# Attention's output projection turned to channels on the partitions, router logits summed before the norm, the residual kept in PSUM, a ninth weight slot

## The chip, the cores and the metric

The kernel runs on one core of one Trainium2 chip. The metric is the device time of one execution in microseconds, the median of three runs. The engines are named as in the profile: PE (TensorE matmul), PEld (its weight load), DVE (VectorE), ACT (ScalarE), POOL (GpSimd), SP (SyncE, which here only issues transfers).

## The reference

A batch of 256 tokens with 1024 channels goes through a first block (gated branches and a feed-forward layer) and then through a second block with attention and a mixture of 32 experts. All data is float32. What the change touches is the end of the attention and all that follows:

```python
    mixed = jnp.concatenate([_rmsnorm(o_dil, g_dil_out[layer]),
                             _rmsnorm(o_sb, g_sb_out[layer])], axis=-1)
    x = x + gate_mix[:, None, :] * (mixed @ w_out[layer])
    h2 = _modulate(_rmsnorm(x, g_ffn[layer]), shift_ffn, scale_ffn).reshape(b * s, d)
    y = _hierarchical_moe(h2, w_group[layer], w_expert[layer],
                          w_gate[layer], w_up[layer], w_down[layer]).reshape(b, s, d)
    x = x + gate_ffn[:, None, :] * y
return _rmsnorm(x, g_final)
```

`o_dil` and `o_sb` are the outputs of two kinds of attention, 8 heads of 64 channels each. `_hierarchical_moe` takes group logits (4) and expert logits (32) of each token from `h2`, picks the best group, in it the two best experts, weighs them by a softmax, and adds `(silu(x @ w_gate) * (x @ w_up)) @ w_down` of those two experts. `_modulate(h, shift, scale)` is `h * (1 + scale) + shift`; `gate_mix`, `shift_ffn` and the others are six rows of 1024 numbers, computed from a condition vector.

## The kernel before, in words

`program` writes one instruction stream for each engine by hand (`tensor`, `scalar`, `vector`, `gpsimd`, `sync`); each engine runs its stream strictly in the order in which it is written and waits on semaphores. Nothing is scheduled by a planner.

Up to the end of the attention the weights come as 127 units of 1 MB (`raw`, four buffers). ACT rounds a unit to a high part (line 971), POOL subtracts to get the low part (line 1961), and PE makes three products of each pair (lines 446 to 448: high by high, high by low, low by high), so one unit of 1024 x 256 weights costs 48 matmuls. There are three buffers (NSP = 3) for the two parts of a unit.

The rows of modulation numbers lie in `ADA`. Sums over partitions (`mc_mm`, line 651) put 16 columns of them on partitions, and the helper `spread` (line 660) copies eight blocks of 512 numbers to all partitions, three blocks ahead of the transposes of X (line 673), four ahead of the norm of the attention's input, and one inside the attention. ACT takes each block back to SBUF (line 1207).

The attention runs in two halves of heads. It ends with the value products of the second half (lines 732 to 734), counted by `dv_mm`; DVE divides by the softmax sums (line 1753), ACT squares all four pieces (line 1312) and takes a root, DVE makes four diagonal matrices (line 1773), PE multiplies them in (line 806), ACT and DVE round the result to `xah` and `xal` (lines 1002, 1399), and PE applies the four units of `w_out_2` token by token (`token_major`). DVE multiplies by the gate and adds to X (lines 1789, 1791). Then follow, one after another: the sum of squares and root of X (ACT 1328), the normed and modulated tokens H2 (DVE 1800, 1803), their transpose (PE 821), the copy to HT (ACT 1332, DVE 1810), the logits (PE 832), the choice of experts (DVE 1815 to 1869), the ranks of the tokens in their experts (PE 839 to 841, DVE 1872, 1875), a selection matrix for four experts (DVE 1886), the gathering of their tokens (PE 857), and the first expert (PE 874).

Each expert's weights are three transfers of 2 MB (`EXPERT_WEIGHTS`: two for gate and up, one for down), 96 in all, into a ring of eight slots of 4096 numbers a partition. SP issues them in order (line 2016). The first eight wait until their memory is free (two on `dv_mm`, two on raw buffers, three on the buffers of parts, the last on H2); each later one waits until the transfer eight places before has been used. An expert x runs as `gate_up(x)`, `turn(x-1)`, `scatter(x-2)`, `down(x-1)` on PE. ACT and DVE each copy a half of an expert's output (lines 1362, 1936), and `scatter` (line 921) adds it to four PSUM banks that stay until the end. Every fourth expert is preceded by the gather of the next four.

After the last expert DVE multiplies the sum by the gate and adds X (lines 1944, 1947), a branch on `FLAG` follows (`general`, the way for experts with over 32 tokens), and a last block takes the norm (ACT 2036, 2038), DVE scales (lines 2048, 2050) and SP stores (line 2057).

Of the kernel before, what the change touches and what calls it, by code (L numbers as in the profile page):

```python
# [9 lines left out]
I32 = mybir.dt.int32  # L10
# [5 lines left out]
D = 1024  # L16
# [10 lines left out]
def constants():  # L27
# [15 lines left out]
    put("iota", np.tile(np.arange(32)[None], (128, 1)))  # L43
# [65 lines left out]
def stream_plan():  # L109
# [57 lines left out]
    for n in range(4):  # L167
        whole("w_out_2", "w_out_2", 256 * n, by_rows)
# [8 lines left out]
    for a in range(len(units)):  # L177
        if units[a].half:
# [7 lines left out]
           ("c_2", 8), ("g_mix_2", 8), ("g_dil_out_2", 4), ("g_sb_out_2", 4), ("g_sgu_v", 8), ("b_sgu_v", 8),  # L186
# [11 lines left out]
def program(nc, I, out, const_at):  # L198
    with ExitStack() as ctx:
# [25 lines left out]
        SM = at("SM", 2392, 640)  # L225
# [13 lines left out]
        def ar(off, n, k=None):  # L239
# [23 lines left out]
              for p in range(2)]  # L263
# [9 lines left out]
        MR = ADA[:, 2048:6144].rearrange("p (k n) -> p k n", k=4)  # L273
# [8 lines left out]
        GF2 = ar(8704, 1024)  # L282
        TMPX = at("tmp4", O_XB, 1024)

        H2 = ar(6144, 2048, 2)
        HT = k8(at("ht", O_XA, 2048))
        SLOT = ([at(f"slot{n}", TOP - 8192 + 4096 * n, 4096) for n in range(2)] +
                [at(f"slot{n + 2}", O_RAW + 4096 * n, 4096) for n in range(5)] + [at("slot7", O_XB, 4096)])
        NS = len(SLOT)
        RT = at("RT", 3032, 72).rearrange("p (t n) -> p t n", t=2)  # L290
        WC = at("WC", 3104, 64).rearrange("p (t n) -> p t n", t=2)
        AS, RK, WL = (at(n, 3168 + 64 * i, 64).rearrange("p (t n) -> p t n", t=2)
                      for i, n in enumerate(("AS", "RK", "WL")))
        FLAG = at("FLAG", 3360, 1, I32)
# [4 lines left out]
        GFI = ar(4096, 1024)  # L299
        YP = [ar(8192 + 1024 * n, 1024) for n in range(2)]  # L300
        HE = [ar(10240 + 128 * n, 128) for n in range(2)]
        XG = [k8(at(f"xg{n}", O_XA + 2048 + 1024 * n, 1024)) for n in range(2)]
# [11 lines left out]
        def tap(k, c):  # L314
# [10 lines left out]
        MC = small(16)  # L325
        mx, den = small(16), small(16)
        mx3, den3 = (v.rearrange("p (t h) -> p t h", t=2) for v in (mx, den))
        sso, sh = small(4), small(2)
        gm, gs = small(2), small(2)
        GE, G1 = small(8).rearrange("p (t g) -> p t g", t=2), small(8).rearrange("p (t g) -> p t g", t=2)  # L330
        hot1, hot2, tmp32 = (small(64).rearrange("p (t g) -> p t g", t=2) for _ in range(3))
        m1, m2, dd = small(2), small(2), small(2)
        ixs = [small(2) for _ in range(3)]
        over, left = small(1), small(1)
        so = small(2)
# [5 lines left out]
        d_ws, d_gmp, d_ada, d_gfp, d_p, d_wr, d_gf2, d_gfi, d_out = (sem(n) for n in (  # L341
            "d_ws", "d_gmp", "d_ada", "d_gfp", "d_p", "d_wr", "d_gf2", "d_gfi", "d_out"))
# [4 lines left out]
                 ("norm3", 4), ("heads", 8))  # L347
# [7 lines left out]
         sbs_mm, sv_mm, di_mm, dt_mm, dv_mm, o_mm, rt_mm, rk_mm, ov_mm, xg_mm, gu_mm, turn_mm,  # L355
         down_mm, y_mm) = (
            sem(n) for n in (
            "n_mm tile0_mm wsum_mm mix_mm mean_mm pool_mm wide_mm xt_mm mc_mm mr_mm sb_mm sbs_mm sv_mm "
            "di_mm dt_mm dv_mm o_mm rt_mm rk_mm ov_mm xg_mm gu_mm turn_mm down_mm y_mm "
# [3 lines left out]
         cond_ok, ffa_ok, pg_ok, qkv_ok, mr_ok, sba_ok, sbe_ok, die_ok, lp_ok, osq_ok, h2s_ok,  # L363
         ht_ok, ge_ok, dd_ok, xga_ok, hsa_ok, ypa_ok, fin_ok) = (
            sem(n) for n in (
            "warm_ok nsq_ok v_ok sig_ok vs_ok u_ok z_ok g_ok sq_ok crs_ok silu_ok vnorm_ok ple_ok post_ok cond_ok "
            "ffa_ok pg_ok qkv_ok mr_ok sba_ok sbe_ok die_ok lp_ok osq_ok h2s_ok ht_ok ge_ok dd_ok xga_ok "
            "hsa_ok ypa_ok fin_ok "
# [4 lines left out]
         od_ok, dga_ok, gf2_ok, h2_ok, htv_ok, route_ok, rk_ok, wl_ok, se_ok, xgv_ok, hsm_ok, he_ok,  # L373
         swt_ok, ypv_ok, y_ok, so_ok) = (
            sem(n) for n in (
            "blank_ok dg_ok vst_ok vn_ok glu_ok tap_ok wst_ok tab_ok mix_ok pools_ok cc_ok cn_ok bra_ok "
            "brc_ok brb_ok az_ok ada_ok ffm_ok mc_ok pg2_ok hf_ok sbm_ok sbw_ok os_ok dim_ok od_ok dga_ok gf2_ok "
            "h2_ok htv_ok route_ok rk_ok wl_ok se_ok xgv_ok hsm_ok he_ok swt_ok ypv_ok y_ok so_ok "
# [7 lines left out]
                                              ("vd0", 1), ("vd1", 1), ("w_out_2", 4)) for n in range(m)]  # L386
# [25 lines left out]
        def tensor(e):  # L412
# [237 lines left out]
            for j in range(16):  # L650
                mm = e.matmul(ps[b][:, j:j + 1], ADA[:, 128 * j:128 * j + 128], ones[:, 0:1], start=True, stop=True)
# [159 lines left out]
            for j in range(4):  # L811
                free[bb[j]] = [(x_ok, X4 + 2 * j + 2)]
# [1357 lines left out]
```

## Time and profile before

| | |
|---|---|
| median of 3 runs | 1229.05 us (1228.92 to 1231.09) |
| profiled execution | 1230.25 us, its span 1228.5 us |
| mean granted clock of PE | 0.943 |
| busy: PE, DVE, ACT, POOL | 86%, 39%, 32%, 40% |
| read from HBM | 340.33 MB, 278 GB/s over the span |
| expert weights | 96 transfers of 2048 KB |

The span runs from the first to the last instruction of the profiled execution. Times such as 763.0 are microseconds from its start. A busy PE is not PE at its peak, since matmuls are pipelined; fp32 matmuls show as two rows each, transposes as one.

### The profile page before, as it was taken

The numbers are of one execution on the slowest core, as the hardware profiler recorded it, in microseconds if no ns is written. First come the engines' busy times: TensorE is split into PE (matmuls) and PEld (weight loads), VectorE is DVE, ScalarE is ACT, GpSimd is POOL, SyncE is SP. The second block draws the span as 40 slices with busy tenths as digits, with TensorE's granted clock in tenths as the row PEclk, the third lists the DMA queues.
The fourth block names the chain that finished last, engine by engine and source line by source line (L and its number), as shares of the span: only waits on it lengthen the run. The fifth ranks groups of instructions, "written<-read, shape, count | busy, mean of one in ns | idle before, by whom it ended". The sixth has DMA issues, their size and how long they took to land. (4 is left out here: it accounts for less than half of the span.)

```text
span 1228.5 us, 19387 instructions
## 1 busy us (share of the span) xinstructions
PE 1059.9 (86%) x8404; PEld 843.4 (69%) x8404; DVE 484.8 (39%) x854; ACT 392.4 (32%) x570; POOL 497.5 (40%) x209
## 2 busy tenths in 40 slices
PE   7999999999799999988999776897778687878774
PEld 6999999999699998767999775443434343434331
DVE  2999913345434646633185443221212121212113
ACT  6345544634444443354475621100000000000002
POOL 6885996676568886964648220000000000000000
PEclk9999999989989999999899886998989998989897
DMA  8543544273458777953323383999999999999991
GB/s 347 206 173 137 200 179 172 78 274 125 168 192 335 284 282 314 372 193 142 108 99 138 154 349 121 429 426 427 428 425 428 427 426 428 426 428 426 427 415 49
DMA packets 34361, 342.66 MB, mean 279 GB/s; under 512 B 3809, under 2 KB 4193, under 8 KB 5729
## 3 DMA queue, kind: packets, MB, share of 16 engines
q1 hardware_dynamic: 32832, 337.56, 68.0%
q10 hardware_dynamic: 1442, 3.84, 0.9%
q8 instruction: 67, 1.10, 0.4%
q14 instruction: 20, 0.16, 0.0%
HBM read 340.33 MB, written 1.05 MB: 278 GB/s over the span
## 5 line engine op out<-in xcount | busy, mean ns | idle before, releaser
L1961 POOL TENSOR_TENSOR spl<-raw,sph 128x1024 fp32r<-128x1024 f32 x204 | 497.0, 2468 | 216.9 <-ACT sph L971 216.8
L971 ACT ACTIVATE sph<-raw 128x1024 fp32r<-128x1024 f32 x204 | 205.6, 1055 | 120.0 <-DMA raw<-in_stream 76.2
L874 PE MATMUL ps<-slot,xg 128*32 128x256 f32 x2048 | 140.4, 426 | 75.5 <-DMA slot<-in_gu 74.4
L446 PE MATMUL ps<-xbh,sph 128*128 128x256 f32 x608 | 178.1, 293 | 13.4 <-DVE xbl L1409 7.8
L447 PE MATMUL ps<-xbl,sph 128*128 128x256 f32 x608 | 176.6, 290 | 0.0
L448 PE MATMUL ps<-xbh,spl 128*128 128x256 f32 x608 | 176.4, 290 | 0.0
L874 PEld LDWEIGHTS ps<-slot,xg 128*32 128x32 f32 x2048 | 71.8, 119 | 144.4 <-DMA slot<-in_gu 66.6
L446 PE MATMUL ps<-xah,sph 128*128 128x256 f32 x512 | 146.7, 287 | 2.4 <-DVE xal L1399 2.1
L447 PE MATMUL ps<-xal,sph 128*128 128x256 f32 x512 | 145.0, 283 | 0.0
L448 PE MATMUL ps<-xah,spl 128*128 128x256 f32 x512 | 145.0, 283 | 0.0
L446 PEld LDWEIGHTS ps<-xbh,sph 128*128 128x128 f32 x608 | 121.3, 200 | 15.4 <-DVE xbl L1409 6.4
L447 PEld LDWEIGHTS ps<-xbl,sph 128*128 128x128 f32 x608 | 121.5, 200 | 0.0
L448 PEld LDWEIGHTS ps<-xbh,spl 128*128 128x128 f32 x608 | 121.3, 200 | 0.0
L921 PE MATMUL ps<-ar,ar 128*128 128x512 f32 x256 | 118.1, 605 | 1.2 <-DVE ar L1936 1.2
L446 PEld LDWEIGHTS ps<-xah,sph 128*128 128x128 f32 x512 | 98.3, 192 | 3.5 <-issue 2.5
L447 PEld LDWEIGHTS ps<-xal,sph 128*128 128x128 f32 x512 | 98.3, 192 | 0.3 <-issue 0.2
L448 PEld LDWEIGHTS ps<-xah,spl 128*128 128x128 f32 x512 | 98.3, 192 | 0.0
L1921 DVE TENSOR_TENSOR ar<-ar,ps 64x256 f32<-64x256 f32 x32 | 13.5, 423 | 205.6 <-ACT ar L1356 205.6
L1429 DVE SCALAR_TENSOR_TENSOR ps<-ar,COL,ps 128x256 f32<-128x256 f32 x232 | 92.1, 481 | 0.0
L1356 ACT ACTIVATE ar<-ps 64x256 f32<-64x256 f32 x32 | 12.1, 377 | 231.5 <-PE ps L874 231.5
L921 PEld LDWEIGHTS ps<-ar,ar 128*128 128x128 f32 x256 | 48.2, 199 | 49.5 <-issue 49.5
L1936 DVE COPY ar<-ps 128x512 f32<-128x512 f32 x32 | 22.1, 691 | 137.0 <-PE ps L906 137.0
(269 smaller groups left out, 1554.5 us busy)
## 6 DMA issues: line engine op xcount, KB each, us to landing
slot<-in_gu SPq DMA_DIRECT2D x64, 2048.0 KB, 34.9
raw<-in_stream SPq DMA_DIRECT2D x127, 1024.0 KB, 4.8
slot<-in_dn SPq DMA_DIRECT2D x32, 2048.0 KB, 37.0
X<-in_x SPq DMA_DIRECT2D x2, 512.0 KB, 4.4
out<-ar SPq DMA_DIRECT2D x2, 512.0 KB, 2.6
cst<-in_cst SPq DMA_DIRECT2D x1, 928.0 KB, 16.0
ar<-in_ws ACTq DMA_DIRECT2D x1, 512.0 KB, 8.2
ar<-in_b_sgu_s ACTq DMA_DIRECT2D x1, 512.0 KB, 11.0
```

Of the source, the lines that this page charges most:

```text
L446: e.matmul(o, sh, mh, start=start, stop=False)
L447: e.matmul(o, sh, ml, start=False, stop=False)
L448: return e.matmul(o, sl, mh, start=False, stop=stop)
L874: mm = e.matmul(ps[b][32 * q:32 * q + 32, 0:256], XG[g % 2][:, k, (x % 4) * 32:(x % 4) * 32 + 32], W[:, q // 2, k % 4, (q % 2) * 256:(q % ...
L921: mm = e.matmul(ps[yb[tt * 2 + nn]][:, :], SWT[x % 2][:, tt * 128:tt * 128 + 128], YP[x % 2][:, nn * 512:nn * 512 + 512], start=(x == 0), ...
L971: e.activation(u.half(SPH[u.n % NSP], h), u.half(RAW[u.slot], h), ACTF.Copy).then_inc(w.up(hi_ok), 1)
L1356: e.activation(HS[x % 2][0:64, :], ps[bank_of["gu", x]][0:64, 0:256], ACTF.Silu)\
L1429: e.scalar_tensor_tensor(out=acc if k < 30 else CVO[:, c, :], in0=CV[:, c, k:k + 256], scalar=tap(k, c), in1=acc, op0=ALU.mult, op1=ALU.add)\
L1921: e.tensor_tensor(h[0:64, :], h[0:64, :], ps[bank_of["gu", x]][64:128, 0:256], ALU.mult)\
L1936: e.tensor_copy(YP[y % 2][:, 512:1024], ps[bank_of["dn", y, 1]][:, :]).then_inc(w.up(ypv_ok), 1)
L1961: e.tensor_tensor(u.half(SPLO[u.n % NSP], h), u.half(RAW[u.slot], h), u.half(SPH[u.n % NSP], h), ALU.subtract).then_inc(w.up(lo_ok), 1)
```

## The change

- **Output projection.** `w_out_2` is now applied with its columns as the stationary side, so the result has channels on partitions, in eight halves of 128 channels (`out_part`). The sb heads get their norm, their diagonal products and their half of the first two units before the last value products; the dilated heads follow after them. The squares of the dilated heads are taken for each half of heads.
- **Residual and norm.** X is transposed ahead of the attention (`xo`, to `XTO`), and DVE makes the new tokens `XTN` in one operation for each half. ACT squares them and scales them by `(1 + scale) * g` (`HTS`), PE sums the squares (`ss`) and the logits straight from `HTS`, one group of 128 channels at a time. The root of the norm is applied to the logits, with the shift's share (`CB`) added. `HTS` is transposed back into `HN` for the gathers, and the shift is added when the gathered tokens are copied.
- **Routing.** Fewer steps; both exponentials are one, and the weights of the two experts are computed behind the first selection matrix.
- **Spreads.** 24 more columns in `mc`, and two spreads (the gate of the experts) in place of eight.
- **Experts.** DVE multiplies both halves of an expert's output by the gate on their way out of PSUM. Sixteen matmuls at x = 3 (`old_tokens`) add `XTN` to the four banks. The final norm is taken from these banks, in the same block, and stored in four pieces; the branch comes after it.
- **Ring.** Nine slots. The slots of the three buffers of parts wait each for one unit of `w_out_2`, the ninth lies in the memory of `xah` and `xal`. `g_final_2` is loaded at x = 3.

The diff, cut to its core:

```diff
+            for n in range(4):
+                b = bank(("xo", n))
+                claim(b)
+                for tt in range(2):
+                    w.wait_ge(x_ok, X3 + 4 * n + 2 * tt + 2)
+                    for k in range(2 * n, 2 * n + 2):
+                        mm = e.transpose(ps[b][:, o:o + 128], X[:, tt, k * 128:k * 128 + 128], ident)
...
+            def out_part(n, ks, start, stop):
...
+                for h in range(2):
...
+                    w.wait_ge(lo_ok, 2 * u.n + h + 1)
+                    for k in ks:
+                        w.wait_ge(act_lo, part_at["heads_s" if k >= 4 else "heads_d"] + 2 * (k % 4 // 2) + 2)
+                        mm = product(ps[b][:, 0:256], H[:, k, c], L[:, k, c], XA[0][:, k, :], XA[1][:, k, :],
+                                     start and k == ks[0], stop and k == ks[-1])
...
+            o_part("heads_s", (2, 3), OS, 2)
             vv("vd0")
             di_turn(0)
             vv("vd1")
             di_values(0)
-            spread(7)
...
             di_turn(1)
+            out_part(0, (4, 5, 6, 7), True, False)
             di_values(1)
+            out_part(1, (4, 5, 6, 7), True, False)
+            o_part("heads_d", (0, 1), OD, 5)
+            out_part(0, (0, 1, 2, 3), False, True)
+            out_part(1, (0, 1, 2, 3), False, True)
...
+            out_part(2, (4, 5, 6, 7, 0, 1, 2, 3), True, True)
+            for k in range(4):
+                logits(k)
+            out_part(3, (4, 5, 6, 7, 0, 1, 2, 3), True, True)
+            for k in range(4, 7):
+                logits(k)
...
             qk("qd1")
+            warm(ACTF.Sqrt)
+            w.wait_ge(os_ok, 4)
...
+            warm(ACTF.Exp)
             qk("kd1")
...
+            for k in range(8):
+                w.wait_ge(x_ok, X4 + k + 1)
+                e.activation(SQ2[k % 2] if k else SQA, XTN[:, k, :], ACTF.Square).then_inc(w.up(hs_ok), 1)
+                e.activation(HTS[:, k, :], XTN[:, k, :], ACTF.Copy, scale=MC[:, 32 + k:33 + k]).then_inc(w.up(hs_ok), 1)
...
+                e.scalar_tensor_tensor(out=XTN[:, k, :], in0=ps[bank_of["w_out_2", k]][:, 0:256],
+                                       scalar=MC[:, 16 + k:17 + k], in1=XTO[:, k, :], op0=ALU.mult, op1=ALU.add)
...
+                if x == 3:
+                    w.wait_ge(y0_mm, 1)
+                    e.dma_start(GFI, I["g_final_2"].partition_broadcast(128)).then_inc(d_gfi, 16)
...
-                if s < 2:
+                if s == 0:
+                    w.wait_ge(half_used, 2 * units[first["vd1"]].n + 2)
+                elif s < 3:
                     w.wait_ge(dv_mm, 2)
-                elif s < 4:
-                    raws_free(2 * s - 4, 2 * s - 3)
-                elif s < 7:
-                    w.wait_ge(half_used, max(2 * u.n + 2 for u in split_order if u.n % NSP == s - 4))
-                elif s == 7:
-                    w.wait_ge(h2_ok, 7)
+                elif s < 5:
+                    raws_free(2 * s - 6, 2 * s - 5)
+                elif s < NS:
+                    w.wait_ge(half_used, 2 * w_out_units[min(s - 4, 3)].n + 2)
```

SP's stream before, where the expert weights begin (the number behind `slot_` is the tensor's; 111 is slot 0, 118 slot 7):

```order
L2016 DMA slot_111<-in_gu 128x4096 [waits dv_mm]
L2016 DMA slot_112<-in_gu 128x4096
L2016 DMA slot_113<-in_gu 128x4096 [waits lo_ok]
L2016 DMA slot_114<-in_gu 128x4096 [waits lo_ok]
L2016 DMA slot_115<-in_dn 128x4096 [waits half_used]
L2016 DMA slot_116<-in_gu 128x4096 [waits half_used]
L2016 DMA slot_117<-in_gu 128x4096 [waits half_used]
L2016 DMA slot_118<-in_dn 128x4096 [waits h2_ok]
L2016 DMA slot_111<-in_gu 128x4096 [waits gu_mm]
```

And with the change (116 is slot 0, 124 slot 8):

```order
L2150 DMA slot_116<-in_gu 128x4096 [waits half_used]
L2150 DMA slot_117<-in_gu 128x4096 [waits dv_mm]
L2150 DMA slot_118<-in_gu 128x4096
L2150 DMA slot_119<-in_gu 128x4096 [waits lo_ok]
L2150 DMA slot_120<-in_dn 128x4096 [waits lo_ok]
L2150 DMA slot_121<-in_gu 128x4096 [waits half_used]
L2150 DMA slot_122<-in_gu 128x4096 [waits half_used]
L2150 DMA slot_123<-in_dn 128x4096 [waits half_used]
L2150 DMA slot_124<-in_gu 128x4096
L2150 DMA slot_116<-in_gu 128x4096 [waits gu_mm]
```

Nine transfers now stand ahead of the first that waits for an expert, and the last two wait for the last unit of `w_out_2`, no more for H2.

PE's stream before, from the transposes of H2 to the first expert (`ht` is HT, `ar_109` H2, `ar_127` the selection matrix):

```order
L821 MATMUL ps<-cst,ar_109 128x128 [waits h2_ok]
L821 MATMUL ps<-cst,ar_109 128x128 x7
L832 MATMUL ps<-cst,ht 128x36 [waits htv_ok,x_ok,ht_ok,d_wr]
L832 MATMUL ps<-cst,ht 128x36 x7
L832 MATMUL ps<-cst,ht 128x36 [waits x_ok]
L832 MATMUL ps<-cst,ht 128x36 x7
L839 MATMUL ps<-AS,cst 128x32 [waits rk_ok,x_ok]
L840 MATMUL ps<-AS,cst 128x32
L841 MATMUL ps<-AS,cst 128x32
L857 MATMUL ps<-ar_127,ar_109 128x128 [waits se_ok]
```

And with the change, from the last sums behind the last unit of `w_out_2` (`ar_111` is HTS, `ar_112` and `ar_114` are squares, `ar_115` is HN):

```order
L888 MATMUL ps<-cst,ar_112 128x1 [waits sqa_ok]
L890 MATMUL ps<-cst,ar_114 128x1 [waits hs_ok]
L888 MATMUL ps<-cst,ar_112 128x1
L890 MATMUL ps<-cst,ar_114 128x1
L873 MATMUL ps<-cst,ar_111 128x36 [waits hs_ok]
L873 MATMUL ps<-cst,ar_111 128x36
L902 MATMUL ps<-cst,ar_111 128x128 x4
L902 MATMUL ps<-cst,ar_111 128x128 [waits route_ok]
L902 MATMUL ps<-cst,ar_111 128x128 x3
...
L909 MATMUL ps<-AS,cst 128x32 [waits rk_ok,x_ok]
L910 MATMUL ps<-AS,cst 128x32
L911 MATMUL ps<-AS,cst 128x32
```

The logits no longer follow a transpose and a copy; the transposes (line 902) now stand behind the logits, beside the choice of experts.

## Rows read from the trace of the kernel before

**Rows 1.** The page's 40 slices of 30.7 us: memory traffic.

```profile
GB/s 347 206 173 137 200 179 172 78 274 125 168 192 335 284 282 314 372 193 142 108 99 138 154 349 121 429 426 427 428 425 428 427 426 428 426 428 426 427 415 49
```

**Rows 2.** Stretches: length, busy of PE, PEld, DVE, ACT, POOL, PEclk, DMA share, GB/s.

```profile
695.00:700.00 5.00, 3.06 (x14) 3.06 (x15) 0.94 (x3) 1.76 (x5) 0.00 (x0) 0.50 1.04 446
738.00:745.00 7.00, 5.49 (x26) 5.35 (x26) 1.38 (x8) 0.05 (x1) 0.00 (x0) 0.50 0.70 294
745.00:763.00 18.00, 8.98 (x75) 8.19 (x79) 8.44 (x34) 2.45 (x5) 0.00 (x0) 0.64 0.00 0
765.00:1190.00 425.00, 338.78 (x3006) 162.32 (x2998) 74.89 (x161) 33.53 (x68) 0.00 (x0) 0.94 1.01 427
```

**Rows 3.** The timeline of SP's queue: start, length, what is issued.

```profile
691.72 23.29 SPq L2016 DMA_DIRECT2D slot<-in_gu  x4
...
732.77 0.33 SPq L2016 DMA_DIRECT2D slot<-in_dn  x1
763.02 2.06 SPq L2016 DMA_DIRECT2D slot<-in_gu  x2
```

**Rows 4.** Waits of PE, 540 to 764 us: total, times, longest.

```profile
PE ps L839 <- DVE AS L1869: 8.3, 1, 8.3
PE ps L821 <- DVE ar L1803: 5.5, 2, 4.5
...
PE ps L806 <- DVE ar L1773: 5.3, 1, 5.3
PE ps L446 <- ACT ar L1207: 2.9, 1, 2.9
...
PE ps L732 <- ACT ar L1284: 1.5, 2, 0.9
```

**Rows 5.** PE's timeline: product pitch, 16 transposing matmuls, 16 sums, the first gather and expert.

```profile
531.29 3.63 PE L651 MATMUL ps<-cst,ar 128*128 128x1 f32 x32
...
574.10 3.84 PE L439 MATMUL ps<-ar,X 128*128 128x128 f32 x32 [0.42 <-DVE ar L1388]
...
650.23 0.28 PE L448 MATMUL ps<-xbh,spl 128*128 128x256 f32 x1
...
651.31 0.28 PE L448 MATMUL ps<-xbh,spl 128*128 128x256 f32 x1
...
754.49 5.56 PE L857 MATMUL ps<-ar,ar 128*128 128x128 f32 x32 [1.20 <-DVE ar L1886]
761.03 1.29 PE L874 MATMUL ps<-slot,xg 128*32 128x256 f32 x20 [0.98 <-DVE xg L1900]
```

**Rows 6.** DVE's timeline from the last value products to the first expert.

```profile
691.72 0.88 DVE L1753 TENSOR_TENSOR ar<-ps,SM 128x256 f32<-128x256 f32 x2 [5.14 <-PE ps L734]
...
701.39 3.22 DVE L1399 SCALAR_TENSOR_TENSOR xal<-ps,COL,xah 128x256 fp32r<-128x256 f32 x6 [0.46 <-ACT xah L1002]
...
743.53 0.20 DVE L1815 COPY RT<-ps 128x36 f32<-128x36 f32 x1 [3.22 <-PE ps L832]
...
753.33 0.23 DVE L1872 SCALAR_TENSOR_TENSOR RK<-ps,AS 128x64 f32<-128x64 f32 x1 [1.64 <-PE ps L841]
```

**Rows 7.** ACT's timeline: a table load, squares, a root, rounding.

```profile
688.76 1.28 ACT L961 ACT_TABLE_LOAD   x1
...
692.64 0.63 ACT L1312 ACTIVATE tmpa<-ar 128x512 f32<-128x512 f32 x1 [2.38 <-DVE ar L1753]
...
700.52 2.62 ACT L1002 ACTIVATE xah<-ps,COL 128x256 fp32r<-128x256 f32 x6 [0.63 <-PE ps L806]
```

**Rows 8.** POOL's timeline: the low parts of the last two units.

```profile
704.17 10.48 POOL L1961 TENSOR_TENSOR spl<-raw,sph 128x1024 fp32r<-128x1024 f32 x4 [15.74 <-ACT sph L971]
```

**Rows 9.** The timeline of the end: last scatter, residual, norm, store.

```profile
1207.94 3.67 PE L921 MATMUL ps<-ar,ar 128*128 128x512 f32 x8 [0.90 <-DVE ar L1936]
...
1219.50 1.06 ACT L2036 ACTIVATE ar<-X 128x1024 f32<-128x1024 f32 x1
...
1224.14 1.28 DVE L2050 SCALAR_TENSOR_TENSOR ar<-X,SM,ar 128x1024 f32<-128x1024 f32 x1
```

More of the change, by code:

```diff
@@ L653, in tensor @@
             free[b] = [(mc_ok, 1)]
-            def spread(*blocks):
-                for j in blocks:
-                    b = bank(("mr", j))
-                    claim(b)
-                    e.matmul(ps[b][:, :], ones, ADA[:, 2048 + 512 * j:2560 + 512 * j], start=True, stop=True)\
-                        .then_inc(w.up(mr_mm), 1)
-                    free[b] = [(mr_ok, j + 1)]
-            spread(0, 1, 2)
             held.clear()
@@ L795, in tensor @@
             di_values(0)
-            spread(7)
+            for j in range(2):
+                b = bank(("mr", j))
+                claim(b)
+                e.matmul(ps[b][:, :], ones, GATE[:, 512 * j:512 * j + 512], start=True, stop=True)\
+                    .then_inc(w.up(mr_mm), 1)
+                free[b] = [(mr_ok, j + 1)]
+            b = bank("cb")
+            claim(b)
+            w.wait_ge(cw_ok, 2)
+            e.matmul(ps[b][:, 0:36], ones, CWS, start=True, stop=True).then_inc(w.up(cb_mm), 1)
@@ L797, in tensor @@
+            free[b] = [(cw_ok, 3)]
+            held.clear()
             di_turn(1)
+            out_part(0, (4, 5, 6, 7), True, False)
             di_values(1)
[L799 to L809 removed]
@@ new lines, in tensor, with logits @@
+            rb = [bank(("rt", tt)) for tt in range(2)]
+            for b in rb:
+                claim(b)
+            held.update(rb)
+            w.wait_ge(d_wr, 16)
+            def logits(k):
+                w.wait_ge(hs_ok, 2 * k + 2)
+                for tt in range(2):
+                    mm = e.matmul(ps[rb[tt]][:, 0:36], HTS[:, k, tt * 128:tt * 128 + 128], WR[:, k, :], start=(k == 0),
+                                  stop=(k == 7))
+                return mm
+            out_part(2, (4, 5, 6, 7, 0, 1, 2, 3), True, True)
@@ L828, in tensor @@
+            mm.then_inc(w.up(ss_mm), 1)
+            free[b] = [(rs_ok, 1)]
+            logits(7).then_inc(w.up(rt_mm), 1)
+            held.difference_update(rb)
             for tt in range(2):
-                b = bank(("rt", tt))
+                free[rb[tt]] = [(route_ok, tt + 1)]
+            for i in range(4):
+                tt, half = i % 2, i // 2
+                b = bank(("hn", i))
                 claim(b)
-                for k in range(8):
-                    mm = e.matmul(ps[b][:, 0:36], HT[:, k, tt * 128:tt * 128 + 128], WR[:, k, :], start=(k == 0),
-                                  stop=(k == 7))
@@ L2090, in _ @@
[L2090 to L2102 removed]
+                    eng.wait_ge(s_x, 4)
```

682 lines of the change are left out of this document (383 added, 299 removed).

## The prediction

> **What bounds the kernel now.** I read the memory traffic by slices first [rows 1]: from slice 26 on it stands at 425 to 429 GB/s until the last slice but one. The stretch from 765 to 1190 us says why [rows 2]: DMA share 1.01 at 427 GB/s, while PE is busy 339 of 425 us. So the expert phase lasts as long as its transfers. One transfer of 2048 KB takes 2.097 MB / 427 GB/s = 4.91 us, an expert 14.7 us; PE needs 339 / (425 / 14.7) = 11.7 us for one.
>
> Before that phase the memory stands still: 294 GB/s from 738 to 745 us and nothing from 745 to 763 us [rows 2]. SP's queue shows it from the other side [rows 3]: eight transfers are issued from 691.7 to 732.8 us, and the ninth only at 763.02 us, when PE has used the first slot. So the end is set by 763.0 us, plus 88 transfers, plus a tail of PE, DVE and ACT work behind the last ones. The chain from the last value products (691.7 us) to 763.0 us is 71.3 us long, and it is what the change cuts. DMA, PE and the chain are worth something only as they move this release, the number of transfers behind it, or the tail.
>
> **Part 1: up to the attention.** The product that waits 2.9 us for a spread's copy on ACT (line 1207) [rows 4] now waits only for its rounded input, some 1.2 us earlier by my count (the second rounded pair is there at 544.3, it started at 545.5). The 24 more sums cost 24 x 3.63 / 16 = 5.4 us of PE [rows 5], but they replace three spreads (0.9 us each) and stand in a time in which PE waited 2.5 us for X anyway; both orders reach the transposes' end within 0.3 us. The residual's 16 transposes (one row each, half of the 3.84 us of the 32 rows [rows 5]) take the place of four spreads. The four copies of them on DVE, 0.7 us each, delay the first diagonal by about 0.2 us. Taken: 1.0 us earlier, bounds 3 earlier and 1.5 later.
>
> **Part 2: inside the attention.** PE is nearly gapless there, so what is added lengthens it. A product matmul has a pitch of (651.31 - 650.23) / 9 = 0.12 us [rows 5], an fp32 one 3.84 / 16 = 0.24 us. Added: 8 diagonal products 1.9 us, one more spread 0.9 us, the 36-column sum 0.2 us, the sb half of the first unit 24 x 0.12 = 2.9 us; 5.9 us in all. The two waits of together 1.5 us for ACT's turned weights [rows 4] are covered by this work. ACT's new root for the sb heads costs two table loads with their first use, 2 x 1.5 us [rows 7], and two squares and a root, 1.8 us; it lies between 656.4 and 666.1 us, where ACT waits for the last key product. What is queued behind is the split of `vd1`, used only at 678 us. Net 4.4 us: the last value products end at 691.7 - 1.0 + 4.4 = 695.1 us. I call this T.
>
> **Part 3: from T to the first release.** PE starts with the sb half of the second unit, 2.9 us, which hides the norm of the dilated heads: division 0.9 [rows 6], a square behind it 0.5 (half the size of [rows 7]), sum, root, reciprocal and two diagonals 1.2 us. Eight diagonal products take 1.9 us, and ACT and DVE round the first pair, 0.9 + 1.0 us [rows 6, 7], while the second is made: the first product can start at T + 5.9. Then (0.12 us each)
> - unit 0's remaining half with a short wait for the second pair: to T + 9.0;
> - unit 1's half 2.9 and unit 2 with 5.8: to T + 17.7;
> - four channel groups of logits, 8 x 0.24 = 1.9, and unit 3, 5.8: to T + 25.3;
> - three groups more, four sums, the last group: 1.4 + 0.8 + 0.5: T + 28.0.
> DVE's and ACT's work on each half (0.5 + 0.8 us) is shorter than PE's 1.4 us for a half until unit 3 has ended, and the sums and logits behind it give the last half its time.
>
> The choice of experts took from 743.5 to 751.7 us with 34 DVE steps; the change needs 20 up to the same point, the larger ones (64 numbers, 0.26 us each) among them: 5.0 us, T + 33.0. Ranks through PE and back 1.65 us [rows 6], selection matrices 0.9: T + 35.6. The gather 5.6 us and the first gate-up half 2.0 us (761.03 to 763.02) are as before [rows 5], but DVE has copied the first half of the tokens while the second is gathered, so the wait of 1.0 us goes: T + 43.2 = 738.3 us. That is 24.7 us before 763.0. What is gone is the norm on tokens, the transposes in front of the logits (waits of 5.5 us [rows 4]), logits at half clock and a third of the choice.
>
> Do the slots fill in time? Slot 0 is issued at about 684, slots 1 and 2 at T, slot 3 when POOL has the low parts of units 1 and 2, T + 4. Slot 4 needs unit 3's low parts. Its buffer is unit 0's, free at T + 7.6 and T + 9.0; ACT needs 1.1 us and POOL 10.48 / 4 = 2.6 to 3.1 us for a half [rows 8]: T + 14.5. Slots 7 and 8 follow unit 3, T + 25.3. At 4.91 us each the ninth has landed at about T + 41.5, 2 us before the release. So the gain of the ninth slot is whole, 87 instead of 88 transfers behind the release, 4.9 us, but nothing more could be had from an earlier release: the transfers themselves would bind 3 us earlier.
>
> A cost: `g_final_2`, 512 KB, was loaded at 736 us, when the memory soon stood idle; now it goes out inside the saturated stream. With three loads in flight the total was 446 GB/s and not more [rows 2], so it takes 0.524 / 427 = 1.2 us from the weights. The Trainium skill says the same under Trainium Kernel Development and Optimization, Key Constraints: transfers of all issuing queues share the same 16 DMA engines and interleave. Were it not so, the sum would be 1.2 us lower.
>
> **Part 4: experts and tail.** `old_tokens` is 16 fp32 matmuls, 3.8 us of PE once, at a time when nine slots stand full; PE has 3.0 us to spare in every expert, and a release may come several transfers late before the queue is empty. DVE's second copy (0.7 us) takes the place of ACT's and lies beside `gate_up`. Both cost nothing while DMA binds. The last scatter starts on the first half 0.9 us earlier. From its end the span now takes 1228.5 - 1211.6 = 16.9 us [rows 9]. After it: two squares from PSUM 1.6, sum, root and reciprocal 0.9, two scalings 1.4 for the first tokens; the second ones' squares begin behind the first root, and the last scaling ends about 5.1 us after the last scatter. The store takes 3.1 us (the last scaling ended at 1225.4 [rows 9]). That is 8.4 us, so with the earlier scatter 9.4 us are gained. The residual, two table loads and the branch are off the path.
>
> **Sum.** 24.7 + 4.9 - 1.2 + 9.4 = 37.8 us. The profiled execution of 1230.25 us becomes 1192.4; it lay 1.2 us above the median of the runs, so the median becomes 1229.05 - 37.8 = 1191.2 us.
>
> **Rivals.**
> A. The slots bind. If the third unit's low parts or the raw buffers come late (unit 3's buffer is free only after unit 0's last product, and ACT reaches its split behind two rounding steps), the ninth slot is not full at the release, and it is worth nothing. For it speaks the idle memory between slots in the kernel before, when the third and fourth transfer waited for POOL and were issued up to 23.3 us after the first [rows 3]. Late by 8 us it gives 4.9 + 1.5 us less: 1197 to 1198.
> B. The clock. After 5.3 us of waiting [rows 4] PE ran at 0.50 of full clock, 1.2 GHz, from 695 to 700 us [rows 2], with a cost of about 2 us. The change takes out three such waits, but it makes a new one of 2.4 us before the attention's norm, and short ones at T + 3 to T + 6. If the output projection or its end ran at the lower level for some time, two or three such ramps and some more wait would cost 4 to 8 us: 1195 to 1199. The Trainium skill, TensorE: Matmul & The Clock Gate, has PE fall to 1.2 GHz behind idle stretches; by that rule alone the gain would grow where waits are removed and shrink at the new ones, and the trace agrees with both.
> C. The change does less than it says: a semaphore wait in PE's or DVE's order (logits on HTS, the bank of the two logit sums freed by DVE) keeps the chain at 55 us or more in place of 43. Against it: each such release lies over 1 us ahead in my count. It gives 1203 or more.
> D. Slower than before. PE becomes the bound of the expert phase: the place is the loop over experts, with two dependent DVE multiplications in front of `scatter` and all else as before. It would take 14.7 + 37.8 / 32 = 15.9 us per expert to lose everything, at 11.7 us of PE work now. Only a lasting lower clock does that, with a mean below 0.94 x 11.7 / 15.9 = 0.69; at 0.5 an expert costs 22 us, and the time is over 1400. Nothing in the trace points to it.
>
> **How the numbers follow.** My forecast has 0.68 (1186 to 1195; the low end is 3 us from part 1 and 2 us from a shorter tail), A 0.10, B 0.13, C 0.06, D 0.03. The range 1184 to 1199 holds the first three with little left out. A measurement of this kernel tells 0.2% (2.5 us) from no change; all cases but D are faster by more, and some of C's far end is not: faster 0.96, same 0.01, slower 0.03.
>
> **What would show it.** The last value products end near 695; the last unit of `w_out_2` near 720; the choice of experts starts near 723; SP issues the first reused slot at 738, less than 5 us after the memory has gone idle; the traffic then stands at 427 GB/s to about 1168; from the last scatter to the end 8.4 us. It would be wrong if the memory goes idle between the first nine slots, if PE waits over 2 us inside `out_part`, or if the traffic in the stream falls below 420 GB/s.

## The result

| | before | after |
|---|---|---|
| median | 1230.07 us (1228.92 to 1234.29) | 1199.39 us (1197.18 to 1201.46) |
| ratio | | 0.9744, 95% interval 0.9713 to 0.9775 |
| profiled execution | 1230.25 us, span 1228.5 | 1200.4 us, span 1198.6 |
| granted clock of PE | 0.943 | 0.953 |

The change gains 30.7 us. The forecast was 37.8 us less, 1191.2 us: the direction is right, and 7.1 us of the gain are missing. The time is 0.4 us above the upper end of the range, 1199, but the kernel before was 1.0 us slower here than in the forecast (1230.07 against 1229.05); as a share of it, 0.9744 lies between the forecast's 0.9692 and the range's end, 0.9755. Rival B (the clock) is the nearest in kind, but most of the loss is at a place that it did not name.

Each ratio below is to the kernel before as it ran beside that version (its medians went from 1230.1 to 1232.3 us), so across groups of runs the ratios compare and the medians do not quite. One execution of `k_best` in a slower state (1483.24 us, granted clock 0.647) is left out of its median.

From the first release on, the kernel behaves as the forecast said. Stretches of the kernel after, with the columns of [rows 2]:

```profile
740.00:745.00 5.00, 5.00 (x27) 5.00 (x27) 2.56 (x6) 0.00 (x0) 0.00 (x0) 0.54 0.98 413
745.00:750.00 5.00, 5.00 (x92) 3.08 (x94) 0.42 (x1) 1.52 (x5) 0.00 (x0) 1.00 0.44 125
750.00:755.00 5.00, 4.19 (x64) 2.18 (x60) 1.14 (x3) 0.38 (x1) 0.00 (x0) 1.00 1.00 426
...
765.00:1160.00 395.00, 315.79 (x2801) 151.97 (x2800) 87.59 (x175) 17.30 (x52) 0.00 (x0) 0.95 1.01 427
```

The memory is idle for some 3 us before 748 us, not for 20 as in [rows 2], and then stands at 427 GB/s again. The first reused slot, in SP's queue after:

```profile
747.42 0.33 SPq L2150 DMA_DIRECT2D slot<-in_gu  x1
749.14 0.33 SPq L2150 DMA_DIRECT2D slot<-in_dn  x1
```

That is 747.4 against 763.0 us [rows 3]: 15.6 us earlier, where 24.7 were forecast. The end of the kernel after, PE's last scatter, DVE's scalings, SP's store:

```profile
1187.11 3.67 PE L1001 MATMUL ps<-ar,ar 128*128 128x512 f32 x8
...
1192.18 1.54 DVE L2081 SCALAR_TENSOR_TENSOR slot<-ps,SM,gfi 128x512 f32<-128x512 f32 x2
...
1192.96 3.49 SPq L2156 DMA_DIRECT2D out<-slot  x4
...
1194.55 1.54 DVE L2081 SCALAR_TENSOR_TENSOR slot<-ps,SM,gfi 128x512 f32<-128x512 f32 x2
```

The last scatter ends at 1190.8 in place of 1211.6 us [rows 9], and 7.8 us follow in place of 16.9. So the span's 29.9 us are 15.6 (release) + 5.2 (from the release to the last scatter's end, 448.6 before, 443.4 after) + 9.1 (tail). All that is missing lies ahead of the release: the other two come out 0.6 us better each than the forecast's 4.6 and 8.5.

And there it lies far ahead, in the step that the forecast took for free. PE's timeline after: the 40 sums (80 rows), the 16 transposes, the first gate product, the attention's norm:

```profile
530.73 14.98 PE L659 MATMUL ps<-cst,ar 128*128 128x1 f32 x80
545.58 3.65 PE L671 MATMUL ps<-cst,X 128*128 128x128 f32 x16
...
550.99 0.55 PE L454 MATMUL ps<-sph,xbh 128*128 128x256 f32 x1 [1.76 <-DVE xbl L1505]
...
581.20 5.26 PE L447 MATMUL ps<-ar,X 128*128 128x128 f32 x32 [2.53 <-DVE ar L1491]
```

Sixteen sums took 3.63 us before [rows 5], so forty should take 9.1; they take 15.0. The stretches of the kernel after show why:

```profile
532.00:534.00 2.00, 2.00 (x16) 2.00 (x16) 1.70 (x2) 0.79 (x4) 2.00 (x2) 0.75 0.42 78
534.00:536.00 2.00, 2.00 (x11) 2.00 (x11) 1.83 (x4) 1.39 (x4) 2.00 (x2) 0.50 0.99 418
...
544.00:546.00 2.00, 2.00 (x11) 2.00 (x11) 0.21 (x2) 0.00 (x0) 0.00 (x0) 0.50 0.00 0
...
551.00:556.00 5.00, 5.00 (x23) 5.00 (x24) 2.49 (x6) 3.75 (x6) 3.40 (x2) 0.50 0.01 2
```

PE and its weight load are busy all the time, and yet the granted clock falls to 0.50, the 1.2 GHz level, 2.3 us after the row of sums has begun; from there the pitch of a row is 0.213 us in place of 0.112. It stays there through the transposes and into the gate products. Before, it was at 1.00 until 546 us.

### The profile page after: what moved, and what is told of

The parts are those of the page before. It is cut to its first block, busy times and chain, and to the rows that moved or that the text cites. A ratio compares the mean times of both kernels' runs of the same rounds, so it can differ in the third digit from the quotient of the medians.

```text
span 1198.6 us, 19625 instructions
## 1 busy us (share of the span) xinstructions
PE 1063.1 (89%) x8498; PEld 853.4 (71%) x8498; DVE 504.5 (42%) x885; ACT 381.8 (32%) x579; POOL 496.2 (41%) x209
## 4 chain that ended last, share of the span: by engine, by line
PE 57%; DMA 25%; DVE 13%; ACT 3%; issue 1%; POOL 1%; DVEq 0%; SPq 0%; ACTq 0%
DMA slot<-in_gu 24%; PE ps L454 13%; PE ps L455 12%; PE ps L456 12%; PE ps L947 5%; DVE ps L1532 5%; PE ps L1001 3%; PE ps L928 2%; PE ps L979 2%; PE ps L447 1%; PE ps L659 1%; DMA raw<-in_stream 1%; DVE ar L1807 1%; DVE xbl L1512 1%; POOL spl L2095 1%
## 5 line engine op out<-in xcount | busy, mean ns | idle before, releaser
L454 PE MATMUL ps<-xbh,sph 128*128 128x256 f32 x608 | 177.3, 292 | 14.1 <-DVE xbl L1512 8.5
L454 PE MATMUL ps<-xah,sph 128*128 128x256 f32 x576 | 165.2, 287 | 3.6 <-DVE xal L1502 3.1
L455 PE MATMUL ps<-xal,sph 128*128 128x256 f32 x576 | 162.9, 283 | 0.0
L456 PE MATMUL ps<-xah,spl 128*128 128x256 f32 x576 | 162.9, 283 | 0.0
L454 PEld LDWEIGHTS ps<-xah,sph 128*128 128x128 f32 x576 | 110.5, 192 | 5.1 <-DVE xal L1502 2.5
L455 PEld LDWEIGHTS ps<-xal,sph 128*128 128x128 f32 x576 | 110.5, 192 | 0.3 <-issue 0.2
L456 PEld LDWEIGHTS ps<-xah,spl 128*128 128x128 f32 x576 | 110.5, 192 | 0.0
L947 PE MATMUL ps<-slot,xg 128*32 128x256 f32 x1024 | 68.5, 417 | 38.5 <-DMA slot<-in_gu 38.5
L947 PE MATMUL ps<-slot,ar 128*32 128x256 f32 x1024 | 68.4, 419 | 33.4 <-DMA slot<-in_gu 33.4
L2063 DVE TENSOR_TENSOR ar<-ps,ar 128x512 f32<-128x512 f32 x64 | 44.3, 692 | 113.3 <-PE ps L979 113.2
L947 PEld LDWEIGHTS ps<-slot,xg 128*32 128x32 f32 x1024 | 35.1, 117 | 73.5 <-DMA slot<-in_gu 33.5
```

The costliest lines, as they stand in the source:

```text
L454: e.matmul(o, sh, mh, start=start, stop=False)
L455: e.matmul(o, sh, ml, start=False, stop=False)
L456: return e.matmul(o, sl, mh, start=False, stop=stop)
L947: mm = e.matmul(ps[b][32 * q:32 * q + 32, 0:256], XG[g % 2][:, k, (x % 4) * 32:(x % 4) * 32 + 32], W[:, q // 2, k % 4, (q % 2) * 256:(q % ...
L2063: e.tensor_tensor(YP[y % 2][:, c], ps[bank_of["dn", y, nn]][:, :], GATE[:, c], ALU.mult)\
```

## The experiments

Theory: a row of products with a single column each, though PE is busy with it, makes the chip take the clock back, and that is the whole miss. Rival: 24 more sums are simply more work than the wait for X can hide.

The executions differ by several microseconds ahead of the sums: the row began anywhere from 528.3 to 535.7 us, mostly since the transfers between 480 and 530 us ran at different rates (from 500 to 510 us 355 GB/s in the kernel after, 277 in `k_best_busy`, 392 in `k_wide_gfi`). So beside the medians I compare three stretches of each trace that such shifts leave alone: from the start of the sums to the first gate product (**S**), from there to the issue of the store (**R**), and from there to the end of the span (**E**). After: S 20.3, R 642.0, E 5.6 us.

**Wide sums in the changed kernel** (`k_wide`).

```diff
-                mm = e.matmul(ps[b][:, j:j + 1], ADA[:, 128 * j:128 * j + 128], ones[:, 0:1], start=True, stop=True)
+                mm = e.matmul(ps[b][:, j:j + 128], ADA[:, 128 * j:128 * j + 128], ones, start=True, stop=True)
```

> The changed kernel, in which each of the 40 sums multiplies by 128 columns of ones and not by one. The sums land in ascending columns, so that a later one writes over all but the first column of an earlier one, and the result is the same. Theory (the clock): 40 single-column products in a row let the granted clock fall to the 1.2 GHz level, and that is where the forecast was missed. Wide products take about as long at full clock (the spreads' fp32 products of 512 columns took 0.9 us, the norm's of 128 columns 0.24 us), so the row of sums lasts 40 x 0.24 = 9.6 us in place of 14.98, the clock from 532 to 551 us stays near 1.00, the first gate product comes at 545 in place of 551.0, the last value products end at 695 to 696 in place of 703.0, and the time is 1191 to 1193 us. Rival (the work alone): 24 more sums are too much work for that place, whatever their width; the row stays at 15 us, the time at 1199.

Measured: 1191.27 us, ratio 0.9662 (0.9633 to 0.9692). Its PE timeline, DVE's first row behind the last value products, SP's first reused slot:

```profile
531.71 9.09 PE L659 MATMUL ps<-cst,ar 128*128 128x128 f32 x80
...
544.76 0.36 PE L454 MATMUL ps<-sph,xbh 128*128 128x256 f32 x1 [1.76 <-DVE xbl L1505]
...
693.26 0.88 DVE L1870 TENSOR_TENSOR ar<-ps,SM 128x256 f32<-128x256 f32 x2 [6.65 <-PE ps L741]
...
737.77 0.33 SPq L2150 DMA_DIRECT2D slot<-in_gu  x1
```

and its stretches:

```profile
534.00:536.00 2.00, 2.00 (x20) 2.00 (x20) 1.86 (x3) 0.46 (x3) 2.00 (x2) 1.00 0.75 270
544.00:546.00 2.00, 1.24 (x9) 1.12 (x9) 1.72 (x5) 2.00 (x6) 0.00 (x0) 1.00 0.00 0
```

A product of 128 columns takes no longer than one of a single column, and with it the clock stays at 1.00. S is 13.05 us, 7.2 less, and in the nine executions with wide sums in the changed kernel it is 12.96 to 13.06. R is 3.3 less: 2.4 in the gate products (25.3 us in place of 27.7), 1.4 in the attention's norm (3.84 in place of 5.26), and 0.5 given back in small pieces behind them. Not all of this need be owed to the width: the gate products took 26.6 to 26.8 us in three other executions with wide sums, and the norm 5.20 (`k_wide_gfi`) and 5.47 us (`k_final`) in two. The whole miss is gone: the ratio falls by 0.0082, some 10 us, and the trace's two stretches by 10.5, by one operand's width.

**Sixteen sums in the changed kernel** (`k_16sums`).

```diff
-            for j in range(40):
-                mm = e.matmul(ps[b][:, j:j + 1], ..., ones[:, 0:1], start=True, stop=True)
+            for j in range(16):
+                mm = e.matmul(ps[b][:, j:j + (25 if j == 15 else 1)], ..., ones[:, 0:25 if j == 15 else 1], start=True, stop=True)
```

> The changed kernel with 16 sums in place of 40, as in the kernel before; the last of the 16 writes the other 24 columns, so 24 modulation numbers of each row are wrong, and only the work is changed. Clock theory, with the forecast's claim that 24 more sums at full clock are hidden behind the wait for X: the row takes 3.6 us, the time is the same as with 40 wide sums within 1 us, 1190 to 1193. If the sums cost something also at full clock, this kernel is faster than the one with wide sums by up to 5.4 us (1186 to 1188). If neither number nor width matters (the loss comes from the transposes and copies of the residual), it stays at 1199.

Measured: 1196.6 us, ratio 0.9722 (0.9695 to 0.9748). This fits none of the three numbers. Its PE timeline and one of its stretches:

```profile
530.61 3.65 PE L659 MATMUL ps<-cst,ar 128*128 128x1 f32 x32
536.90 1.11 PE L671 MATMUL ps<-cst,X 128*128 128x128 f32 x4 [2.64 <-DVE X L1697]
539.75 3.18 PE L671 MATMUL ps<-cst,X 128*128 128x128 f32 x12 [1.74 <-DVE X L1697]
```

```profile
536.00:538.00 2.00, 1.10 (x4) 0.71 (x4) 1.72 (x5) 0.21 (x3) 0.56 (x1) 0.50 0.31 45
```

Here the row ends at full clock, PE waits 2.64 us, and the clock has fallen by the time the transposes start; before, the three spreads stood between the sums and that wait, and the clock held. S is 14.1 and R 640.6: 1.0 and 1.9 us worse than forty wide sums. So the 24 more sums are hidden at full clock, as forecast (with wide ones PE still waited 0.23 us for X), and as filling they even help. The rest of the difference, 3.4 us, lies behind the issue of the store: E is 9.1 us in place of 5.6. DVE's last scaling ends 3.1 us behind that issue in both. The difference is in PE's sequencer, at the branch on `FLAG` over `general`. PE's branch in `k_wide`, then here (480 and 3912 ns):

```profile
L2168 PEldq COMPARE_BRANCH  x1: 480/480/480, 1188.3 to 1188.3; - x1
```

```profile
L2168 PEldq COMPARE_BRANCH  x1: 3912/3912/3912, 1190.1 to 1190.1; - x1
```

The branch lasts 0.4 to 0.5 us in all six kernels whose PE stream is as long as that of the change, and 3.6 to 4.0 us in all five with fewer or more matmuls in it (this one and the four with added products below). So 3.4 us of this run's miss come neither from what the sums cost PE nor from the clock.

**Forty sums in the kernel before** (`b_sums40`, `b_wide40`): `range(16)` becomes `range(40)`; in the second also the wide operand.

> The kernel before, with 40 single-column sums in place of 16 (the other 24 are used by nobody), its spreads kept. Clock theory: the row takes 15 us in place of 3.63, the clock falls to 0.5 after about 2 us of it, the first gate product comes 7 to 9 us later than 545.5, and as the chain to the first release sets the end, the time is 1236 to 1239 us. Rival (the work alone): 5.4 us more of PE, of which 2.5 to 3.5 lie in the wait for X: 1231 to 1232.

> The kernel before, with 40 sums of 128 columns in place of 16 single-column ones. Clock theory: the row takes 9.6 us at full clock, the three spreads behind it end at about 543 where X is there at 540.6, and the time is 1231 to 1233 us, some 5 us below the same kernel with single-column sums. Rival (any 24 more sums at this place): the same time as with 40 single-column sums.

Measured: 1238.24 us, ratio 1.0046 (1.0032 to 1.0060), and 1232.26 us, ratio 1.0001 (0.9987 to 1.0016). The sums and the first gate product of the one, then of the other:

```profile
531.15 13.26 PE L651 MATMUL ps<-cst,ar 128*128 128x1 f32 x80
...
554.11 0.36 PE L446 MATMUL ps<-sph,xbh 128*128 128x256 f32 x1 [2.95 <-ACT ar L1207]
```

```profile
534.32 9.09 PE L651 MATMUL ps<-cst,ar 128*128 128x128 f32 x80
...
550.68 0.36 PE L446 MATMUL ps<-sph,xbh 128*128 128x256 f32 x1 [2.94 <-ACT ar L1207]
```

S was 14.2 us before; it is 23.0 with single columns and 16.4 with wide ones. The work alone costs 2.2 us by S (the median doesn't show it), the width of one column 6.6 more, and the medians differ by 6.0. The row of single columns takes 13.26 us and not the expected 15, since the clock falls 4.1 us into it and not after 2. The cause of the loss, a long row of single-column products, is shown in both kernels, by adding it and by taking it away. Why the chip takes the clock back at such a row, and why after 2.3 us in one kernel and 4.1 in the other, is not shown.

**Without the ninth slot** (`k_wide_8slots`), on wide sums: `slot8` is left out of the list of slots.

> The changed kernel with sums of 128 columns, and without the ninth slot. Forecast's step: the first release stays at 737.8 us, the memory is idle one transfer longer before it, and 88 instead of 87 transfers follow: 4.9 us slower than with nine slots, a ratio to the kernel before that is 0.0040 higher than 0.9662. The rival (the ninth slot comes too late to be worth anything): the same time.

Measured: 1193.27 us, ratio 0.9713 (0.9691 to 0.9735), 0.0051 above wide sums alone (the intervals just overlap). The release comes at 735.86 us, 44.5 us behind the last value products as with nine slots, and the second half of the last expert's gate and up products starts 429.4 us after it in place of 424.6: 4.8 us, as forecast. To the store it is only 3.4 us more, because that half took 1.93 us here and 3.34 with nine slots, at a falling clock.

**Late `g_final_2`** (`k_wide_gfi`).

```diff
-                if x == 3:
+                if x == 31:
                     w.wait_ge(y0_mm, 1)
                     e.dma_start(GFI, I["g_final_2"].partition_broadcast(128)).then_inc(d_gfi, 16)
```

> The changed kernel with sums of 128 columns, in which the 512 KB of g_final_2 are loaded behind the last expert's gate and up products and not at the fourth expert, so out of the saturated stream. Forecast's step: they take 0.524 MB / 427 GB/s = 1.2 us from the weights, so from the first release to the end of the transfers it takes 1.2 us less, and the span is 1.2 us shorter. Rival (the load fits into gaps between packets of the weights): no difference in that stretch. The medians can hardly tell 0.1%; the trace's stretch does.

Measured: 1188.70 us, ratio 0.9666 (0.9651 to 0.9680). From the first reused slot (736.63) to the store (1181.10) it takes 444.47 us, with the early load 445.68: 1.21 us, the forecast's 1.2. The next two kernels show it again: 445.73 us with the early load (`k_wide_old`), 444.48 with the late one (`k_best`). The median's ratio doesn't show it.

**Diagonals earlier** (`k_wide_old`), **and both** (`k_best`).

```diff
-            for n in range(3):
-                old(n)
+            old(0)
             diagonal(2, 0, ss3, DG)
-            old(3)
+            old(1)
             diagonal(2, 1, ss3, DG)
+            for n in (2, 3):
+                old(n)
```

> The changed kernel with sums of 128 columns, in which DVE makes the two diagonals of the attention's norm behind the first and the second copy of the residual, and not behind the third and fourth. In the changed kernel PE waits 2.53 us for the diagonal ahead of that norm. If the copies are what delays it, the wait falls by 0.7 to 1.5 us, all later steps and the release come that much earlier, and the time falls by about as much. Rival (the wait is for the square and root of X on ACT): the wait stays at 2.5 us, the time too.

> The changed kernel with all three: sums of 128 columns, the diagonals earlier, g_final_2 late. If the effects add, 1.9 to 2.7 us below the kernel with wide sums alone: a ratio to the kernel before of 0.964 to 0.966. Rival (the effects don't add, since the transfers bind from the third slot on): 0.9662 as with wide sums alone.

Measured: 1192.65 us, ratio 0.9688 (0.9671 to 0.9705), and 1190.12 us, ratio 0.9664 (0.9649 to 0.9680). PE's wait ahead of the norm, in the first, and DVE's step ahead of the diagonal:

```profile
574.19 3.84 PE L447 MATMUL ps<-ar,X 128*128 128x128 f32 x32 [2.04 <-DVE ar L1491]
...
573.65 0.16 DVE L1484 RECIPROCAL SM<-SM 128x1 f32<-128x1 f32 x1 [1.20 <-ACT SM L1068]
```

The wait is 2.04 in place of 2.53 us: 0.5 us, under what I expected. DVE now waits 1.20 us for ACT's root, so the rest of PE's wait belongs to ACT. R is 638.4 and 637.2, against 638.7 for wide sums alone: by the trace the one edit brings 0.3 us and both together 1.5. By the medians they bring nothing.

**PE kept busy in its waits** (`k_best_gather`, `k_best_busy`). Products of the ones matrix, read by nobody; the last hunk is in `k_best_busy` alone:

```diff
             b = bank("rk")
             claim(b)
+            for _ in range(13):
+                e.matmul(ps[b][:, 0:128], ones, ones, start=True, stop=True)
             w.wait_ge(rk_ok, 1)
...
-                w.wait_ge(se_ok, 2 * g + 2)
...
+                    if g == 0 and i == 0:
+                        for _ in range(4):
+                            e.matmul(ps[b][:, 0:128], ones, ones, start=True, stop=True)
+                    w.wait_ge(se_ok, 2 * g + 2)
...
+                    if x == 31 and k == 4:
+                        spare = bank("spare")
+                        claim(spare)
+                        for _ in range(10):
+                            e.matmul(ps[spare][:, 0:128], ones, ones, start=True, stop=True)
```

> The changed kernel with sums of 128 columns, the diagonals earlier and g_final_2 late, and in addition 13 products of the matrix of ones while PE waits 3.2 us for the choice of experts, and 4 more while it waits 0.97 us for the first selection matrix. Nobody reads them. Without them the clock is at the 1.2 GHz level from the ranks to the middle of the first gather, which takes 6.79 us for 32 rows. Theory (what the clock gives back is worth time on the chain): the gather takes 3.7 to 4.2 us, the first reused slot is issued 2 to 3 us earlier behind the last value products (42 in place of 44.5 us), still at or behind the landing of the ninth slot, and the time is 2 to 2.5 us less, 1188 us. Rival: the transfers bind there already, or the products' bank or PE's own queue delays the ranks: release less than 1 us earlier, time as before or worse.

> The same, with 10 such products more, into a spare bank, while PE waits 2.9 us for the second half of the last expert's gate and up weights. Without them that half runs 2.8 to 3.4 us at a falling clock where it took 1.93 us in the kernel with eight slots. Theory: the half takes 1.93 us, the tail is 0.9 to 1.4 us shorter, 1187 us. Rival: the products end behind the landing and cost up to 1 us.

Measured: 1192.96 us, ratio 0.9672 (0.9644 to 0.9699), and 1192.48 us, ratio 0.9664 (0.9641 to 0.9688). The gather in `k_best`, then the products and the gather in `k_best_gather`, then the products and the last expert's half in `k_best_busy`:

```profile
732.00 6.79 PE L928 MATMUL ps<-ar,ar 128*128 128x128 f32 x32 [0.97 <-DVE ar L2008]
```

```profile
727.86 3.07 PE L909 MATMUL ps<-cst 128*128 128x128 f32 x26
...
732.97 3.84 PE L933 MATMUL ps<-ar,ar 128*128 128x128 f32 x32
```

```profile
1159.55 2.50 PE L953 MATMUL ps<-cst 128*128 128x128 f32 x20
1162.48 1.93 PE L957 MATMUL ps<-slot,xg 128*32 128x256 f32 x32 [0.43 <-DMA slot<-in_gu]
```

The gather falls from 6.79 to 3.84 us, and from the issue of the ninth slot to that of the tenth it takes 14.9 in place of 17.9 us; to the store 460.0 in place of 462.4, since the last half took 3.46 in place of 2.77 us there; with that half kept at full clock, 458.5. The mechanism works as expected, 3.9 us in all by this stretch. The memory then no longer goes idle ahead of the release (at least 279 GB/s in every microsecond from 736 to 742 us in `k_best_busy`; 49, 49 and 0 GB/s from 738 to 741 us in `k_best`), so by this a still earlier release would gain nothing more.

The medians show none of it, and the branch at the end says where most of it goes: E is 8.9 and 8.8 us in place of 5.6. PE's branch in `k_best`, then in `k_best_gather` (480 and 3747 ns), and the instruction transfer in the latter's time:

```profile
L2169 PEldq COMPARE_BRANCH  x1: 480/480/480, 1190.0 to 1190.0; - x1
```

```profile
L2174 PEldq COMPARE_BRANCH  x1: 3747/3747/3747, 1188.6 to 1188.6; - x1
...
q8 instruction: 1, 0.02, 2.1%
```

While each long branch lasts, a transfer of 16 KB of instructions begins; in no short one does it. So PE may wait there for its next instructions, and whether it has to may depend on how many stand before the branch; that is an inference, and no run tests it.

**The same without the early diagonals** (`k_final`), **and once more with them** (`k_busy_again`).

> The changed kernel with sums of 128 columns, g_final_2 late and the 27 products of ones that fill PE's waits, but with the diagonals where the change has them. In the four kernels with the diagonals earlier the row of sums started at 533.9 to 535.7 us, in the five forms of the change without that edit at 528.3 to 531.7: something between 480 and 530 us, long before the edited place, cost 3 to 4 us, and the medians showed no gain. Theory (it comes with this edit, by the place of the instructions or the data in memory): the row starts at 528 to 532 us here, and the time is 1186 to 1188.5 us, a ratio to the kernel before of 0.963 to 0.965. Rival (chance from one execution to the next): the start lies anywhere between 528 and 536, and the median at 1190 to 1192, as with the diagonals earlier.

> The same kernel with the diagonals earlier (run a second time), for the comparison on one chip. Theory: the row of sums starts at 534 to 536 us again, the median is 2 to 4 us above that of the kernel without the edit. Rival (chance): it may start at 528 to 532 this time, and the two medians agree within 1 us.

Measured: 1190.02 us, ratio 0.9655 (0.9628 to 0.9681), and 1191.16 us, ratio 0.9662 (0.9633 to 0.9692). The row of sums began at 532.5 and at 534.5 us; R is 634.8 and 634.1 us (633.4 in `k_best_busy`). All five profiled executions with the early diagonals began it at 533.9 to 535.7, all six without that edit at 528.3 to 532.5, but the kernel before with wide sums, which has no such edit either, began at 534.3. The two medians agree within their intervals. Whether the edit costs some 3 us at a place long before it, or chance does, **stays open**. R is 3.9 to 5.3 us shorter in these three than with wide sums alone, but E is longer by 3.1 to 3.5 (8.8, 8.8 and 9.2 in place of 5.6 us), since PE's branch lasts 3.6 to 4.0 us. From the start of the sums to the end they are only 0.7 to 2.1 us shorter, which the medians cannot tell.

Every version of the change with wide sums and nine slots beats both kernels; `k_wide` does it with one operand (0.9662, its interval below that of the change), and none of the others can be told from it. The interval of `k_wide_8slots` overlaps that of the change.

## Why the prediction was right or wrong

**Part 1 failed.** The step was that the 24 more sums cost 24 x 3.63 / 16 = 5.4 us of PE and are hidden, since both orders "reach the transposes' end within 0.3 us"; the part was taken 1.0 us earlier, with a late bound of 1.5. Measured: the fourth round of products behind the attention's norm starts at 596.7 us in place of 588.2, 8.5 later. From the start of the sums the transposes end after 11.3 us before, after 18.5 with the change, and after 11.3 with wide sums. So the count of work was sound: at full clock S is 13.05 us in place of 14.2, a gain of 1.1. What failed was to price each of 40 sums at 3.63 / 16, the price in a row of 16. I had a rival for the clock, but looked for it behind waits only.

The Trainium skill, TensorE: Matmul & The Clock Gate, Part 1, has the half clock come with an idle PE and the full one with a busy PE. The trace does not agree for the sums: PE was busy for all 15.0 us, and ran at 0.50 for most of them. The measurement decides: at this place a busy PE did not keep the clock, and the width of the products did.

**Part 2 was a little too dear.** From the fourth round of products behind the norm to the last value products: 103.5 us before, 106.3 after, 106.6 with wide sums. That is 2.8 to 3.1 more, against a net 4.4. Together with part 1: the last value products end at 703.05 in place of 695.1 us, 9.5 late by the first part and 1.6 early by the second.

**Part 3 held.** From there to the first reused slot 44.4 us, forecast 43.2, before 71.3. The output projection begins 6.6 us in (forecast 5.9), the choice of experts starts 29.0 us in (28.0), the ranks come back and the selection is made at 35.9 (35.6), gather and first half take 8.5 (7.6). The last difference is the clock again: the gather was taken at 5.6 us, as before, and took 6.52, at 0.50 for all but its last 0.9 us; with PE kept busy it is 3.84. With wide sums the release is at 737.8 us, and the forecast said 738.3; that is in part luck, since the last value products end 1.9 us earlier there than forecast (693.2 us), and the release comes 1.3 us later behind them (44.5).

**Slots, ninth slot, GFI held.** The memory moves 369 GB/s or more in every 5 us from 705 us until the ninth slot is full, and is idle at 745 us, 42 us in (forecast 41.5). The ninth slot is worth 4.8 us (4.9) up to the last half of gate and up products, and 3.4 to the store, since that half then runs at a falling clock. The early `g_final_2` costs 1.21 us (1.2). That the transfers would bind with a release 3 us earlier held too: with the added products the release came 3.0 us earlier, and the memory's idle time was gone.

**Part 4 held.** From the last scatter's end 7.8 us (8.4). From the release to the last scatter's end 5.2 us less; the terms say 4.9 - 1.2 + 0.9 = 4.6.

**The rivals.** A did not come: the traffic of the nine transfers had all but ended 2 us before the release (115, 66 and 0 GB/s in the three microseconds from 745 us). B was right in kind and nearly in size (1195 to 1199), and mostly wrong in place: of its new waits, the one ahead of the norm came (2.53 us, and the norm took 5.26 us in place of 3.84), but the output projection ran at a clock of 1.00 from 705 to 735 us. C did not come: the chain is 44.4 us long, 1.2 over the forecast. D: PE was busy 315.8 of 395 us in the stream at a clock of 0.95, far from binding.

## What to carry to other kernels

Price a long row of single-column matmuls (40 here; 16 kept the clock) at the lower clock level, and what follows it closely too, even where PE has no gap; widening the moving operand cost nothing here and gave some 10 us back. On a chain, look at the clock of each short piece behind a wait: products that nobody reads, put into a known wait, can bring the next piece to full speed. And when an edit is worth less than the spread between executions, compare stretches of the trace with fixed ends, and say that the median doesn't show it. Let these stretches reach to the end of the span, sequencers included: here 3.2 of 3.9 us won on the chain were lost at a branch that no edit touched.

## What was not expected of the hardware

- The granted clock fell to 0.50 while PE and its weight load were busy without a gap: 2.3 us into 40 single-column fp32 products (14.98 us for 80 rows; 9.09 at 128 columns with the clock at 1.00), and 4.1 us into the same row in the kernel before.
- A single-column fp32 product and one of 128 columns take the same time at full clock: 3.63 us for 16, 9.09 us for 40.
- The same norm of 32 rows behind the same wait of 2.53 us took 3.84 us in three executions and 5.2 to 5.5 in three others; behind a wait of 2.04 us it took 3.84 in all five.
- One branch on PE's sequencer took 0.37 to 0.48 us in six kernels and 3.6 to 4.0 us in the five whose PE stream had 48 rows fewer, or 34 or 54 more, out of 8498; the branch and its place in the source were the same.
